# Gate row operations placed between the chunks of the first query block, gate columns copied ahead of a gating, and carried decays brought by transfers

## What is computed

```python
z = rmsnorm(x, norm1_g) @ w_in             # u | q | k | v | o | gates
qk = silu(centred_dwconv(z[q and k], conv_w, conv_b))     # three taps
logi, logf = gates, log_sigmoid(gates)     # 4 heads, two directions
# chunkwise mLSTM, in both directions
b = cumsum(logf)                           # within a chunk
m_t = max(b + m_prev, max(Dlog))
C_new = exp(bT + m - m_new) * C + exp(ml - m_new) * C_loc     # carried state
h = (w_inter * q @ C_prev + scores @ v) / max(|den|, exp(-m_t))
...
x = x + [pool_mixer(u) | rmsnorm(h) * sigmoid(o)] @ w_out
x = x + expert_choice_ffn(rmsnorm(x))      # 16 experts, SwiGLU
```

## Time and profile before

| what | us |
|---|---|
| median of 3 runs (1902.0 to 1903.52) | 1902.82 |
| the profiled execution | 1902.86 |
| its span, first to last instruction | 1900.9 |
| PE busy | 1808.0 |
| DVE busy | 472.3 |
| ACT busy | 386.4 |
| mean granted clock of PE, of full speed | 0.974 |

### The profile page before, as it was taken

One profiled execution on the slowest core, in us unless ns is written; L12 is line 12 of the kernel. 1 busy time (PEld: TensorE's weight loads), 2 busy tenths in 40 slices (PEclk: granted clock), 3 DMA queues, 4 the chain that ended last, 5 costly groups with the idle time before them and its releaser, 6 DMA issues. The chain is left out here.

```text
span 1900.9 us, 24306 instructions
## 1 busy us (share of the span) xinstructions
PE 1808.0 (95%) x10094; PEld 1462.1 (77%) x10094; DVE 472.3 (25%) x987; ACT 386.4 (20%) x869; POOL 210.6 (11%) x235
## 2 busy tenths in 40 slices
PE   8997999999999998999769999999999999999996
PEld 5544555875555694555469999999999999999996
DVE  3461111652011472147620111011111011111014
ACT  3334231644021362122200000000000000000005
POOL 0070010230100022000000100011110011110010
PEclk9997999999999998999779999999999999999998
DMA  6110200111000312623426866676866777866685
GB/s 190 48 48 1 64 34 28 34 63 55 7 27 28 118 54 87 213 81 118 159 76 239 280 220 225 243 262 236 278 225 224 240 264 233 286 220 224 238 270 210
DMA packets 147787, 292.21 MB, mean 154 GB/s; under 512 B 7512, under 2 KB 32776, under 8 KB 147732
## 3 DMA queue, kind: packets, MB, share of 16 engines
q1 hardware_dynamic: 140868, 269.28, 40.6%
q0 software_dynamic: 6864, 22.17, 4.6%
HBM read 260.13 MB, written 31.31 MB: 153 GB/s over the span
## 5 line engine op out<-in xcount | busy, mean ns | idle before, releaser
L1730 PE MATMUL bank<-arena 128*128 128x164 f32 x4096 | 581.3, 303 | 0.0
L1730 PEld LDWEIGHTS bank<-arena 128*128 128x128 f32 x4096 | 572.9, 190 | 0.3
L1749 PE MATMUL bank<-arena 128*128 128x164 f32 x2048 | 295.3, 303 | 0.0
L1749 PEld LDWEIGHTS bank<-arena 128*128 128x128 f32 x2048 | 286.5, 190 | 0.0
L1106 PE MATMUL bank<-arena 128*128 128x512 f32 (+1 forms) x576 | 216.4, 538 | 7.1 <-ACT arena L618 7.1
L1106 PEld LDWEIGHTS bank<-arena 128*128 128x128 f32 x576 | 110.7, 193 | 111.5 <-issue 94.1
L1639 DVE TENSOR_TENSOR arena<-bank,arena 128x328 f32<-128x328 f32 x64 | 31.9, 499 | 584.5 <-ACT arena L1579 584.5
L1071 PE MATMUL bank<-arena 128*128 128x384 f32 x528 | 171.2, 485 | 0.0
L1423 PE MATMUL bank<-arena 128*128 128x512 f32 x352 | 161.5, 617 | 1.1 <-issue 0.7
L1071 PEld LDWEIGHTS bank<-arena 128*128 128x128 f32 x528 | 99.8, 189 | 70.4
L1579 ACT ACTIVATE arena<-bank 128x328 f32<-128x328 f32 x64 | 28.4, 443 | 558.9 <-PE bank L1730 558.9
(11 more groups left out here) (213 smaller groups left out, 1445.9 us busy)
## 6 DMA issues: line engine op xcount, KB each, us to landing
arena<-in_w_up SPq DMA_DIRECT2D x32, 2048.0 KB, 12.8
arena<-in_w_down SPq DMA_DIRECT2D x32, 2048.0 KB, 11.2
arena<-in_w_gate SPq DMA_DIRECT2D x32, 2048.0 KB, 8.0
arena<-in_w_in SPq DMA_DIRECT2D x8, 1536.0 KB, 6.4
arena<-in_x_sample SPq DMA_DIRECT2D x14, 512.0 KB, 6.2
arena<-decay_rows SPq DMA_DIRECT2D x22, 256.0 KB, 3.5
residual<-arena SPq DMA_DIRECT2D x11, 512.0 KB, 5.2
ffn_in<-arena SPq DMA_DIRECT2D x11, 512.0 KB, 3.6
```

The costliest lines, as they stand in the source:

```text
L1730: last = pe.matmul(ps[2 * w + fp % 2][:, a * SLOTS:(a + 1) * SLOTS], ring[2 * (fp // 2) + w][:, k, f * P:(f + 1) * P], xeT[:, k, :], start ...
L1749: last = pe.matmul(ps[4 + dp % 2][:, a * SLOTS:(a + 1) * SLOTS], ring[4 + dp // 2][:, k, dt * P:(dt + 1) * P], hidT[:, k, :], start=k == 0 ...
```

## The change

Three things are rewritten. `gate_rows_rest` becomes `gate_rows(step)`, and its steps 0, 1 and 2 stand each ahead of one chunk's copy in the first group's `conv_centre`, step 3 (with `rows_ready`) behind that group's centre taps. The copies of the gate columns move ahead of the second group's `silu`. The key ("sp",) and its 32 products and copy are gone: SP stores `S1` to DRAM and loads it back into `spc`, broadcast over partitions, by eight transfers, for which DVE waits before the state phase.

```diff
@@ bank_plan
-                keys += [("rc", i) for i in range(NT)] + [("sp",)]
+                keys += [("rc", i) for i in range(NT)]
@@ SP, after load_w(3)
                         sp.wait_ge(rows_ready, 1)
                         for d in range(2):
                             sp.dma_start(neg_d[:, 2 - 2 * d:4 - 2 * d, :], negM[d * BW:d * BW + 4, :]).then_inc(rows_out_d, 16)
+                            sp.dma_start(carry_d[d, :, :], S1[d * BW:d * BW + 4, :]).then_inc(carry_out, 16)
+                        sp.wait_ge(carry_out, 32)
+                        for p in range(2):
+                            for j, parts, h in ((0, slice(0, P), 0), (1, slice(0, 64), 0), (1, slice(64, P), 1), (2, slice(0, P), 1)):
+                                sp.dma_start(spc[parts, 6 * p + j:6 * p + 6:3, :],
+                                             carry_d[:, 2 * p + h, :].unsqueeze(0).to_broadcast([parts.stop - parts.start, 2, NT])).then_inc(carry_in, 16)
@@ ACT
-                def gate_rows_rest():
-                    st.settle()
-                    rows_out(R[2], R[6], ACT.Exp)
-                    rows_out(R[3], R[5], ACT.Exp, scale=-1.0)
-                    rows_out(negM, R[4], ACT.Copy, scale=-1.0)
-                    st.settle()
-                    rows_out(R[5], R[0], ACT.Copy, bias=LN_SCALE)
-                    st.settle()
-                    act.sem_inc(rows_ready, 1)
+                def gate_rows(step):
+
+                    if step == 0:
+                        st.settle()
+                        rows_out(R[2], R[6], ACT.Exp)
+                    if step == 1:
+                        rows_out(R[3], R[5], ACT.Exp, scale=-1.0)
+                    if step == 2:
+                        rows_out(negM, R[4], ACT.Copy, scale=-1.0)
+                        st.settle()
+                    if step == 3:
+                        rows_out(R[5], R[0], ACT.Copy, bias=LN_SCALE)
+                        st.settle()
+                        act.sem_inc(rows_ready, 1)
@@ ACT, conv_centre
                     for c, (lo, hi) in enumerate(CHUNKS):
+                        if n == 0:
+                            gate_rows(c)
@@ ACT, main loop
-                gate_rows_rest()
                             conv_centre(p, w, j)
+                            if (p, w, j) == (0, 0, 0):
+                                gate_rows(3)
+                            if (p, w, j) == (0, 0, 1):
+                                for i in range(NT):
+                                    evac(("rc", i), cols[:, i, :, :], lambda b: b[:, 0:4 * NR].rearrange("p (a n) -> p a n", a=4))
...
                             silu(p, w, j)
-                            if (p, w, j) == (0, 0, 1):
-                                for i in range(NT):
-                                    evac(("rc", i), cols[:, i, :, :], lambda b: b[:, 0:4 * NR].rearrange("p (a n) -> p a n", a=4))
-                                evac(("sp",), spc[:, :, :], lambda b: b[:, 0:12 * NT].rearrange("p (a n) -> p a n", a=12))
@@ DVE, before the state phase
-                        b, k = plan[("sp",)]
-                        dve.wait_ge(free[b], k)
+                        dve.wait_ge(carry_in, 128)
@@ PE, gate_columns
-                    b = bank(("sp",))
-                    for pp in range(2):
-                        for d in range(2):
-                            for j in range(3):
-                                a = ((pp * 2 + d) * 3 + j) * NT
-                                for h in ((0,), (0, 1), (1,))[j]:
...
-                                    last = pe.matmul(ps[b][parts, a:a + NT], ident[0:NR, r:r + 1].to_broadcast([NR, n]),
-                                                     S1[:, :], start=True, stop=True)
-                    last.then_inc(full[b], 1)
```

More of the change, by code:

```diff
@@ L142, in encoder_program @@
     neg_d = nc.dram_tensor("decay_rows", (2, 4, T), F32, kind="Internal").ap()
+    carry_d = nc.dram_tensor("carry_rows", (2, 4, NT), F32, kind="Internal").ap()
     ctx = ExitStack()
@@ L247, in encoder_program @@
         rows_out_d, decay_masked, decay_taken = sem("rows_out_d"), sem("decay_masked"), sem("decay_taken")
+        carry_out, carry_in = sem("carry_out"), sem("carry_in")
         decay_in = [sem(f"decay{s}_in") for s in range(RING_E)]
@@ L744, in _ @@
                         act.activation(o_gate, o_gate, ACT.Sigmoid).then_inc(o0_open, 1)
-                        read_out(act, ("sp",))
+                        read_out(act, ("rc", NT - 1))
                     for i in range(NT):
@@ L1081, in gate_columns @@
                         last.then_inc(full[b], 1)
-                    b = bank(("sp",))
-                    for pp in range(2):
-                        for d in range(2):
-                            for j in range(3):
-                                a = ((pp * 2 + d) * 3 + j) * NT
-                                for h in ((0,), (0, 1), (1,))[j]:
-                                    parts = slice(0, P) if j != 1 else slice(64 * h, 64 * h + 64)
-                                    n = P if j != 1 else 64
-                                    r = row(d, 2 * pp + h)
-                                    last = pe.matmul(ps[b][parts, a:a + NT], ident[0:NR, r:r + 1].to_broadcast([NR, n]),
-                                                     S1[:, :], start=True, stop=True)
-                    last.then_inc(full[b], 1)
                 pe.wait_ge(masks_done, 1)
```

## The result

| | before | after |
|---|---|---|
| median, us (lowest to highest) | 1902.87 (1902.00 to 1903.52), 4 runs | 1875.05 (1874.31 to 1877.27), 4 runs |
| profiled execution / its span | 1902.86 / 1900.9 | 1875.08 / 1873.1 |
| ratio, 95% interval | | 0.9856 [0.9839, 0.9873] |

The ratio is a gain of 27.4 us (24.2 to 30.6). Two later comparisons of the same two kernels, on two chips, gave 0.9886 [0.9866, 0.9905] (1896.52 and 1876.86) and 0.9859 [0.9839, 0.988] (1901.78 and 1874.48). So the change is clearly faster, by 18 to 31 us, and how much was measured depended on when and where.

The account below looks back on a forecast made before the run. TensorE, busy 1808.0 of 1900.9 us, was taken as the bound. Savings of 7.1 + 2.5 + 7.8 + 0.9 + 5.2 + 1.7 = 25.2, less 2.7 for the clock, gave 1902.9 - 22.5 = 1880.4 us; range 1876.5 to 1883.5.

Parts of the forecast that it names:

- The wait before the second block: TensorE's 7.13 us idle between first and second block would go, the first bank being free 1.3 us early.
- The second block at full clock: Without the gap ahead of it, the second block would take 17.67 us instead of 20.20, saving 2.5 us.
- The wait for `cols`: Before the fourth tile's gate column transposes, TensorE would wait 1.65 us instead of 9.43, saving 7.8 us.
- L1091, the transfers: Dropping the 32 small products that broadcast the carried decays would save 5.2 us, the transfers replacing them costing nothing.
- The clock behind the gate columns: TensorE's clock would fall at the transposes' end or the third block's start, giving back 2.7 us (1.4 to 4.0).
- Rival 1: The clock stays up behind the gate columns, as 1.65 us idle is short: 1877.7 us, chance 0.18.
- Up to the values: The net gain, 25.2 us less 2.7 for the clock, was put at 22.5 us, all won before the values.
- one sum serves both: Profiled execution (1902.86 us) and median of the runs (1902.82) agree, so the gain was taken from 1902.9 for both.
- 1.2 us for the two later falls: Allowance in the range's low end, below rival 1, for two later clock falls priced at 1.4 and 3.1 us.
- Later rows earlier by one constant: Sign that everything after the changed stretch, released by TensorE's progress, would move earlier by the same amount.
- The high end's terms: Range's top, 1883.5 us: forecast plus dearest clock (+1.3) and a first wait of up to 1.5 us.
- Rivals 2 to 4: Second block still waits (1882 to 1884, chance 0.07); slow decay loads matter (0.02); another wait replaces one (about 1890, 0.03).

Follow-up runs that it names:

- second trace of before: The kernel before, unaltered, profiled once more: 1895.72 us, with 236.47 us from output projection to experts.
- this part alone: The kernel before with only the carried decays by transfers: 1894.84 us, ratio to before 0.9978.
- removing the light stretch with its wait: The changed kernel with the gate columns' transposes given out one tile behind each chunk of the third block and first keys: medians 1875.38, then 1874.33 us.
- the gate columns alone: The kernel before with only the copies to `cols` and `spc` moved ahead of the second block's gating: 1889.2 us, ratio to before 0.9948.
- the first kernel with added products: The changed kernel with extra `ident` by `ident` products behind the state phase and in the output projection's last two tiles: 1871.30 us, ratio to before 0.9842.

## Why the prediction was wrong, point by point

- **The wait before the second block.** Right: gone, the bank free at 137.8 with 1.3 us to spare, as worked out. The second block at full clock: right.
- **The wait for `cols`.** Forecast 1.65 in place of 9.43; 1.53 in all four traces of the changed kernel. Right.
- **L1091, the transfers.** Right: the third block's end came 4.97 us earlier with this part alone (6.07 against the second trace of before), forecast 5.2, and nobody waited for the loads. A load took 7.6 us to land (the median), where I had taken 3.5; they were issued by 157.7, and the cover (SP not needed before 182) made it cost nothing.
- **The clock behind the gate columns.** Right in kind: it fell, at 161.0, after a wait of only 1.53 us. The Trainium skill, TensorE: Matmul & The Clock Gate, "HAM oscillation — how this bites in real kernels", asks only that idle gaps between bursts of matmuls be short; this trace and the fall after 0.51 us idle speak against it. Rival 1, that the clock stays up, did not occur; removing the light stretch with its wait removed the fall. In size: third block over 17.67 and 32 transposes over 2.69 give 3.1, 2.8, 1.5 and 3.0 us in the four traces, forecast 2.7.
- **Up to the values** the forecast was 22.5 and the two first traces differ by 22.46, of which 0.22 lie ahead of the first block. So the mechanism of this stretch was right. That the size fits to 0.1 us is luck: column A differs by 22.2 to 25.0 us between the traces of before and after, by 23.3 on average.
- **What failed** is "one sum serves both" and the term "1.2 us for the two later falls". I took the base of 1902.8 as the kernel's time since the shown runs agreed within 1.5 us, and saw no row that said otherwise. But a stage of 240 us that the change doesn't touch varies by 8.5 us with the clock, and the first trace of before has it at its longest, 244.93. The changed kernel's first trace had 239.83, and the difference of 5.1 is what the forecast missed (0.26 more are in the experts). "Later rows earlier by one constant" failed with it: the offset is 22.46 us at the values and 27.54 at the experts' first product. In the terms of the sum, the two later falls gave 3.3 us where I had allowed 1.2, and 1.8 more came from the stage's first large products (1.0) and its last transposes (0.8), which I had put at nothing. Had I priced the two later falls as I priced the near one (1.4 and 3.1 for the large products alone, and 0.4 + 1.6 for the transposes and 16-column products of the first one, by its rows at half clock), the low end would have been up to 6.5 us below rival 1's 1877.7, not 1.2, and the range would have held. The measured 1875.05 lies nearer to rival 1's time than to the forecast, but not for rival 1's reason. (The high end's terms add up to 1883.2, not 1883.5.)
- **Rivals 2 to 4** did not occur.

What decides in which of its lengths an execution finds the middle stage stays open. The runs of before near 1896 and near 1902 came in different shares (17 of 30 below 1899 on one chip, 3 of 22 in the other comparisons), and nothing in the traces says why.

## What to carry to other kernels

An edit's price is best read between marks in the trace, not from totals: cut both traces at the same instructions, and a stage that the change doesn't touch but that differs is the noise of that trace. Look at the granted clock of every stage of the base before taking its time as fixed, and price each fall at its full cost for the range, with some 8 us of 240 here. Work that waits in a strict order on one engine is worth giving out between the pieces that another engine waits for, but not in pieces so small that the change of shape (0.2 us a piece here) eats the gain.

## What the runs showed of the hardware

- TensorE's clock can fall to half with no long wait: once it fell at 897.06, after 1.04 us of transposes, 1.02 of large products, 0.51 idle and 1.93 of 16-column products; and it fell in all six traces that have the 36-column transposes with a single wait of 1.53 (four of the changed kernel, the gate columns alone, the first kernel with added products). The first of these rows stood in another kernel without a fall, and so did the wait of 2.08 in the second trace of before: the rows alone don't decide it.
- The same code took 236.47 and 244.93 us in two executions of one kernel, DVE's and ACT's busy times being equal to 0.2 us, at mean clocks of 0.92 and 0.88.
- A chunk of 512-column products that follows four small transposes took 7.07 us to the next group against 6.87 by its share of an undisturbed block (52.84 / 3 us).
- The eight loads of `spc` (rows of 44 bytes spread over partitions), issued one behind the other in 4.81 us, took 4.4 to 8.1 us from issue to landing, with a median of 7.6 for the 11 KB ones and 6.7 for the 5.5 KB ones.
